# A decoder step on one core: key chunk and memory in quarters, logits between projections, a reordered top-k

## The reference

```python
m = rmsnorm(mem, g_mem)                    # 256 memory tokens
k = m @ w_k; v = m @ w_v
x = x + mixer(rmsnorm(x, g_mix), ...)      # spatial gate and short conv
x = x + cross_attn(rmsnorm(x, g_xattn), k, v, w_q, w_xo)
h = rmsnorm(x, g_moe)
logits = h @ w_router + b_router           # 32 experts
top_logit, top_e = lax.top_k(logits, 4); gates = softmax(top_logit)
# for each expert e: tokens gathered, then
gate, up = split(xb @ w1[e] + b1[e])
y = ((clip(up, -7, 7) + 1) * min(gate, 7) * sigmoid(1.702 * min(gate, 7))) @ w2[e] + b2[e]
x = x + sum over the 4 experts of gates * y
y = rmsnorm(x, g_final)
```

## Time and profile before

| what | value |
|---|---|
| median of 3 runs | 1243.08 us (1242.49 to 1243.96) |
| profiled execution | 1242.54 us, its span 1240.6 us |
| TensorE busy (PE) | 1162.7 us, 94% |
| VectorE busy (DVE) | 283.3 us, 23% |
| ACT busy | 166.0 us, 13% |
| moved by DMA | 458.5 MB, 370 GB/s on the mean |
| mean granted TensorE clock | 0.993 |
| chain that ended last | PE 50%, DMA 44%, DVE 4%, issue 2% |

### The profile page before, as it was taken

One profiled execution on the slowest core, in us unless ns is written; L12 is line 12 of the kernel. 1 busy time (PEld: TensorE's weight loads), 2 busy tenths in 40 slices (PEclk: granted clock), 3 DMA queues, 4 the chain that ended last, 5 costly groups with the idle time before them and its releaser, 6 DMA issues.

```text
span 1240.6 us, 14166 instructions
## 1 busy us (share of the span) xinstructions
PE 1162.7 (94%) x5620; PEld 618.5 (50%) x5620; DVE 283.3 (23%) x603; ACT 166.0 (13%) x267; POOL 29.6 (2%) x53
## 2 busy tenths in 40 slices
PE   8999999999999999999999999999999899989995
PEld 7888887775444444344444433333444343334433
DVE  5214532342111111111122111111111111111115
ACT  2011011021111111111111112111111111111112
POOL 1000000010000000000000000000000000000000
PEclk9999999999999999999999999999999999999998
DMA  9953334945999999999999999999999999999991
GB/s 372 409 176 136 130 143 169 427 189 213 417 428 427 426 428 428 427 427 427 427 428 427 428 427 427 428 427 429 427 428 427 426 429 427 428 428 426 429 402 57
DMA packets 37833, 458.53 MB, mean 370 GB/s; under 512 B 5744, under 2 KB 5744, under 8 KB 7056
## 3 DMA queue, kind: packets, MB, share of 16 engines
q1 hardware_dynamic: 35424, 454.11, 87.3%
q10 hardware_dynamic: 2352, 3.54, 0.8%
HBM read 454.41 MB, written 3.23 MB: 369 GB/s over the span
## 4 chain that ended last, share of the span: by engine, by line
PE 50%; DMA 44%; DVE 4%; issue 2%; SPq 0%; ACT 0%; DVEq 0%; ACTq 0%
DMA ring<-in_w_gu 43%; PE ps L1148 19%; PE ps L925 15%; PE ps L1195 6%; PE ps L943 2%; PE ps L1103 1%; PE ps L1123 1%; DVE arena L851 1%; PE ps L1178 1%; DMA ring<-in_w_k 1%; PE ps L1011 1%; PE ps L1042 1%; PE ps L1051 1%; PE ps L1021 1%; DVE arena L860 1%
## 5 line engine op out<-in xcount | busy, mean ns | idle before, releaser
L1148 PE MATMUL ps<-ring,arena 128*64 128x512 f32 x2048 | 456.3, 598 | 40.5 <-DMA ring<-in_w_gu 31.5
L1148 PEld LDWEIGHTS ps<-ring,arena 128*64 128x64 f32 x2048 | 144.7, 138 | 346.9 <-issue 279.9
L1195 PE MATMUL ps<-ring,arena 128*64 128x512 f32 x1024 | 226.8, 595 | 12.4 <-DVE arena L863 12.4
L830 DVE TENSOR_TENSOR resid<-resid,ps 128x264 f32<-128x264 f32 x128 | 51.2, 426 | 724.3 <-PE ps L1123 724.3
L925 PE MATMUL ps<-arena,ring 128*128 128x264 f32 (+1 forms) x832 | 186.6, 386 | 3.2 <-DMA ring<-in_w_k 1.8
L925 PEld LDWEIGHTS ps<-arena,ring 128*128 128x128 f32 x832 | 157.4, 190 | 30.8 <-DMA ring<-in_w_k 2.4
L1195 PEld LDWEIGHTS ps<-ring,arena 128*64 128x64 f32 x1024 | 70.7, 137 | 153.1 <-issue 127.9
L1103 PE MATMUL ps<-arena 128*128 128x256 f32 x432 | 99.0, 380 | 0.9 <-DVE arena L612 0.9
L545 ACT ACTIVATE arena<-ps 128x1024 f32<-128x1024 f32 x32 | 32.8, 1024 | 448.9 <-PE ps L1148 448.9
L1103 PEld LDWEIGHTS ps<-arena 128*128 128x128 f32 x432 | 82.6, 197 | 8.3 <-DVE arena L612 1.2
L1123 PE MATMUL ps<-arena 128*128 128x264 f32 x256 | 72.5, 396 | 0.0
(11 more groups left out here) (190 smaller groups left out, 419.5 us busy)
## 6 DMA issues: line engine op xcount, KB each, us to landing
ring<-in_w_gu SPq DMA_DIRECT2D x128, 2048.0 KB, 23.8
ring<-in_w_dn SPq DMA_DIRECT2D x64, 2048.0 KB, 20.4
ring<-in_w_in SPq DMA_DIRECT2D x10, 1024.0 KB, 28.3
ring<-in_kc SPq DMA_DIRECT2D x8, 1024.0 KB, 4.8
ring<-in_vc SPq DMA_DIRECT2D x8, 1024.0 KB, 4.9
ring<-in_w_v SPq DMA_DIRECT2D x4, 1024.0 KB, 24.7
ring<-in_w_out SPq DMA_DIRECT2D x4, 1024.0 KB, 5.4
ring<-in_w_q SPq DMA_DIRECT2D x4, 1024.0 KB, 4.8
```

Of the source, the lines that this page charges most:

```text
L830: TTN(resid[:, m, :], resid[:, m, :], ps[:, 6 + m % 2, 0:T], ALU.add).then_inc(c_added, 1)
L1148: last = mm(ps[64 * h:64 * h + 64, n, :], xg[:, cur, k, SLOTS * i:SLOTS * i + SLOTS], w[:, at:at + 512], start=(k == 0), stop=(k == KT - 1))
L1195: last = mm(ps[64 * h:64 * h + 64, 4, :], hid[:, k, :], w[:, at:at + 512], start=(k == 0), stop=(k == KT - 1))
```

## The change

The first key chunk comes in four quarters of two feature tiles, issued by SP; the memory comes in four quarters too, issued by ACT. TensorE makes key tiles 0 and 1 together, a quarter at a time. Seven warming matmuls stand in place of twelve. The router product of tile m - 1 stands behind attention output tile m. VectorE adds the square of tile m right behind its scaling. In the top-k, the scan starts from the count of larger logits, two steps are one, and the mask for rows that hold no token is replaced by a threshold of 1e30 in `top8`; slot numbers start at one, and the subtraction of one from the rank is gone. VectorE makes the one-hot matrix by token tiles, then the iteration count, and the gates after that; ACT's exponential stands behind its copies. TensorE loads the iteration count behind the first gather, and waits for the last copy of the gather only ahead of the third unit of the first expert (u == 3 of 0 to 3).

```diff
-            for half in range(2):
-                sp.dma_start(mem_raw[:, 4 * half:4 * half + 4, :], mem_t[:, 4 * half:4 * half + 4, :]).then_inc(mem_in[half], 16)
-                sp.dma_start(ring[:, 0, 1024 * half:1024 * half + 1024],
-                             w_k[0, :, 1024 * half:1024 * half + 1024]).then_inc(landed[0] if half else half_landed, 16)
+            for part in range(4):
+                sp.dma_start(ring[:, 0, 512 * part:512 * part + 512],
+                             w_k[0, :, 512 * part:512 * part + 512]).then_inc(landed[0] if part == 3 else part_landed[part], 16)
...
-            step(nc.gpsimd.iota(slot_i[:], pattern=[[1, SLOTS]], base=0, channel_multiplier=0))
+            step(nc.gpsimd.iota(slot_i[:], pattern=[[1, SLOTS]], base=1, channel_multiplier=0))
...
+            step(nc.gpsimd.memset(top8[:, 2, :], 1e30), top_filled)
...
+            for part in range(4):
+                act.dma_start(mem_raw[:, 2 * part:2 * part + 2, :], mem_t[:, 2 * part:2 * part + 2, :]).then_inc(mem_in[part], 16)
...
             for half in range(2):
-                act.wait_ge(mem_in[half], 16)
+                act.wait_ge(mem_in[2 * half], 16)
+                act.wait_ge(mem_in[2 * half + 1], 16)
...
-                if n == 3:
-                    act.wait_ge(ex_in, 1)
-                    nc.scalar.activation(ex[:], ex[:], ACT.Exp).then_inc(ex_out, 1)
                 act.wait_ge(grp, G[("htok", n)] + 1)
                 nc.scalar.activation(h_tok[0:rows, n // 2, 512 * (n % 2):512 * (n % 2) + 512], bank(("htok", n))[0:rows],
                                      ACT.Copy, scale=rstd_tok[0:rows, n // 2:n // 2 + 1]).then_inc(tok_copied, 1)
+            act.wait_ge(ex_in, 1)
+            nc.scalar.activation(ex[:], ex[:], ACT.Exp).then_inc(ex_out, 1)
             act.wait_ge(late_zero, 5)
...
-                dve.wait_ge(mem_in[k // 4], 16)
+                dve.wait_ge(mem_in[k // 2], 16)
...
-                if m:
-                    add_squares(sq, m - 1, 12)
-            add_squares(sq, KT - 1, 12)
+                add_squares(sq, m, 12)
...
+            dve.wait_ge(top_filled, 1)
             for t in range(TT):
-                ins = nc.vector.max(top8[:, t, :], lg[:, t, :])
+                rows = P if t < 2 else NS
+                ins = nc.vector.max(top8[0:rows, t, :], lg[0:rows, t, :])
                 ins.then_inc(dve_step, 1)
             steps[0] += TT
             dve.wait_ge(dve_step, steps[0])
-            TTN(ex[:], lg[:], top8[:, :, 0:1].to_broadcast([P, TT, NE]), ALU.subtract).then_inc(ex_in, 1)
             fourth = top8[:, :, TOPK - 1:TOPK].to_broadcast([P, TT, NE])
-            link(TTN(gt[:], lg[:], fourth, ALU.is_gt))
-            link(TTN(eq[:], lg[:], fourth, ALU.is_equal))
+            TTN(gt[:], lg[:], fourth, ALU.is_gt).then_inc(dve_step, 1)
+            TTN(eq[:], lg[:], fourth, ALU.is_equal).then_inc(dve_step, 1)
+            steps[0] += 2
+            dve.wait_ge(dve_step, steps[0])
             link(nc.vector.tensor_reduce(cnt3, gt[:], AX.X, ALU.add))
-            link(TS(cnt3, cnt3, -1.0, float(TOPK), ALU.mult, ALU.add))
             for t in range(TT):
-                ins = (nc.vector.tensor_tensor_scan(cum[:, t, :], ones[:, 0:NE], eq[:, t, :], 0.0, ALU.mult, ALU.add))
+                ins = nc.vector.tensor_tensor_scan(cum[:, t, :], ones[:, 0:NE], eq[:, t, :], cnt3[:, t:t + 1],
+                                                   ALU.mult, ALU.add)
                 ins.then_inc(dve_step, 1)
             steps[0] += TT
             dve.wait_ge(dve_step, steps[0])
-            link(TTN(cum[:], cum[:], bc(cnt3, 2, [P, TT, NE]), ALU.is_le))
-            link(TTN(eq[:], eq[:], cum[:], ALU.mult))
-            link(TTN(gt[:], gt[:], eq[:], ALU.add))
-            TTN(gt[:], gt[:], bc(valid[:], 2, [P, TT, NE]), ALU.mult).then_inc(sel_ready, 1)
+            link(STT(eq[:], cum[:], float(TOPK), eq[:], ALU.is_le, ALU.mult))
+            TTN(gt[:], gt[:], eq[:], ALU.add).then_inc(sel_ready, 1)
+            TTN(ex[:], lg[:], top8[:, :, 0:1].to_broadcast([P, TT, NE]), ALU.subtract).then_inc(ex_in, 1)
             dve.wait_ge(sel_ready, 1)
+            b = filled("rank", 128)
+            link(STT(rank[:], b[:, 0:96].rearrange("p (a e) -> p a e", a=TT), 1.0, gt[:], ALU.add, ALU.mult))
+            for t in range(TT):
+                TTN(hot(p_hot)[:, t], slot_no[:].unsqueeze(1).to_broadcast([P, 4, SLOTS]),
+                    rank[:, t, 0:4].unsqueeze(2).to_broadcast([P, 4, SLOTS]), ALU.is_equal).then_inc(first_p if t < 2 else p_built, 1)
+            nc.vector.tensor_reduce(cmax, b[:, 96:128], AX.X, ALU.max).then_inc(emptied, 7)
+            dve.wait_ge(emptied, G["rank"] + 1)
+            link(TTN(over, limits[:], cmax.to_broadcast([P, 4]), ALU.is_lt))
+            link(nc.vector.tensor_reduce(nover, over, AX.X, ALU.add))
+            TS(iters[:], nover[0:1, :], 4.0, 4.0, ALU.mult, ALU.add).then_inc(iters_ready, 1)
             dve.wait_ge(ex_out, 1)
...
-            link(STT(rank[:], b[:, 0:96].rearrange("p (a e) -> p a e", a=TT), 1.0, gt[:], ALU.add, ALU.mult))
-            TS(rank[:], rank[:], -1.0, None, ALU.add).then_inc(rank_ready, 1)
-            dve.wait_ge(rank_ready, 1)
-            build_p(0)
-            nc.vector.tensor_reduce(cmax, b[:, 96:128], AX.X, ALU.max).then_inc(emptied, 7)
-            dve.wait_ge(emptied, G["rank"] + 1)
-
-            link(TTN(over, limits[:], cmax.to_broadcast([P, 4]), ALU.is_lt))
-            link(nc.vector.tensor_reduce(nover, over, AX.X, ALU.add))
-            TS(iters[:], nover[0:1, :], 4.0, 4.0, ALU.mult, ALU.add).then_inc(iters_ready, 1)
...
-            for _ in range(12):
+            for _ in range(7):
                 mm(ps[:, 7, 0:P], ones[:], ones[:], start=True, stop=True)
-            for m in range(KT):
-                project("w_k", m, lambda k: mem[:, k, :], "k", (mem_ready, 0) if m == 0 else None)
-                if m == 1:
-                    pe.wait_ge(const_ready, CONSTS)
-                    sum_squares("mem_ssq", 1, NMEM, 2)
+            first_keys = ring[:, 0, :].rearrange("p (k n) -> p k n", k=KT)
+            for part in range(4):
+                pe.wait_ge(landed[0] if part == 3 else part_landed[part], 16)
+                pe.wait_ge(mem_ready, 2 * part + 2)
+                for m in range(2):
+                    for k in (2 * part, 2 * part + 1):
+                        last = mm(bank(("k", m))[:, 0:NMEM], first_keys[:, k, P * m:P * m + P], mem[:, k, :],
+                                  start=(k == 0), stop=(k == KT - 1))
+                    if part == 3:
+                        last.then_inc(grp, 1)
+            pe.wait_ge(const_ready, CONSTS)
+            sum_squares("mem_ssq", 1, NMEM, 2)
+            for m in range(2, KT):
+                project("w_k", m, lambda k: mem[:, k, :], "k")
...
+            def logits(k):
+                pe.wait_ge(h_ready, 2 * KT + k + 1)
+                return mm(bank("lg")[0:NE, 0:T], router[:, k, :], h_fm[:, k, :], start=(k == 0), stop=(k == KT - 1))
+
             for m in range(KT):
                 project("w_xo", m, lambda k: o_fm[:, k, :], "xo")
-            b = begin("lg")
-            for k in range(KT):
-                pe.wait_ge(h_ready, 2 * KT + k + 1)
-                last = mm(b[0:NE, 0:T], router[:, k, :], h_fm[:, k, :], start=(k == 0), stop=(k == KT - 1))
-            last.then_inc(grp, 1)
+                if m == 1:
+                    begin("lg")
+                if m:
+                    logits(m - 1)
+            logits(KT - 1).then_inc(grp, 1)
...
-            def gather(b, n):
+            def gather(b, n, first=False):
 
                 for half in range(2):
                     for t in range(TT):
+                        if first:
+                            pe.wait_ge(p_built if t == 2 else first_p, 1 if t == 2 else t + 1)
                         last = mm(b[:, 256 * half:256 * half + 256], h_tok[:, t, 256 * n + half:256 * n + 255 + half:2], p_hot[:, t, :],
                                   start=(t == 0), stop=(t == TT - 1))
                 return last
 
-            pe.wait_ge(p_built, 1)
             pe.wait_ge(late_zero, 5)
             pe.wait_ge(tok_copied, 6)
+            pe.wait_ge(first_p, 1)
             for n in range(4):
-                gather(begin(("ga", n)), n).then_inc(grp, 1)
+                gather(begin(("ga", n)), n, n == 0).then_inc(grp, 1)
+                if n == 0:
+                    pe.wait_ge(iters_ready, 1)
+                    end = pe.value_load(iters[0:1, 0:1], min_val=4, max_val=20)
             pe.wait_ge(bdn_in, 16)
-            pe.wait_ge(emptied, NG)
+            pe.wait_ge(emptied, NG - 1)
...
-            pe.wait_ge(iters_ready, 1)
-            end = pe.value_load(iters[0:1, 0:1], min_val=4, max_val=20)
...
+                        if j == 0 and u == 3:
+                            pe.wait_ge(emptied, NG)
```

21 lines of the change are left out of this document (6 added, 15 removed).

## The result

| kernel | median, lowest to highest | ratio of this to before, 95% interval |
|---|---|---|
| before, nine runs beside it | 1245.09 us, 1242.49 to 1247.94 | |
| changed, nine runs | 1253.30 us, 1249.07 to 1254.60 | 1.0063, 1.0051 to 1.0075 |

The changed kernel is slower. The profiled executions took 1253.3 and 1242.54 us, with spans of 1251.6 and 1240.6: 11.0 us between them, where the medians are 8.2 apart. The profiled execution of before is one of its quickest; what sets its spread of 5 us is not settled here.

A forecast was written before the change was run, and what follows sets the result against it. TensorE was taken to bound the front, DMA the expert loop. Head +0.3, tail -0.2 and clock +1.3 gave +1.4: 1243.9 us for the profiled execution, 1244.5 for the median, range 1241.8 to 1247.0.

The forecast's parts named there:

- The frame: Whole kernel: DMA bounds the expert loop, so the end is the loop's start plus a constant, moving one for one.
- memory's sum of squares: Head: its input is ready at 15.57 against TensorE's 15.33, so it starts 0.3 us later.
- half clock in the key tiles behind it: Head: not in the forecast; a rival had the clock fall after the 2.6 us wait, +1.5, 1246.0, chance 0.12.
- router products interleaved: Tail: same total for the products, but a new stall at the end makes the sum of squares 0.6 us later.
- shorter top-k, to the ranks: Tail, VectorE: instructions gone ahead of the selection save 1.1 us.
- gates and their transpose ahead of the gather: Tail: gates come after the one-hots, and their transpose holds up the gather; +2.4 us.
- half clock in the gather: Tail: TensorE's 3.5 us standstill halves the clock for 1.8 to 2.4 us of gather; +1.3 us.
- hole ahead of the loop: Between gather and expert loop: the 2.11 us hole goes, with count load and last copy hidden.
- the landing of the last memory quarter: Head: the last quarter lands at 10.2 to 11.4 us, taken as 10.6.
- memory rows starve: Head rival: ACT's queue gets the parameters' share, TensorE waits 3 to 5 us; 1246.5 to 1249.5, chance 0.10.
- The stall and the late squares: End of the attention output: last router product waits for VectorE, and the sum of squares comes 0.6 us later.
- the conditions named as proof against the forecast: Sum ready before 14, gather starting before 277, or a hole staying at the count's load.

The follow-up runs named there:

- h_act: Kernel before with only the new head (memory in quarters on ACT's queue, keys in quarters, seven warming matmuls), old tail: 1249.40 us, ratio 1.0042.
- t_lg: Changed kernel with the old head, router products back behind the last projection and the earlier adding of squares taken back: 1243.51 us, ratio 0.9987.
- t_two: Changed kernel with the old head, router products 0 to 5 together behind attention output tile 6, the others behind tile 7: 1245.23 us, ratio 1.0001.
- t_only: Changed kernel with the head of the kernel before (halves on SP, twelve warming matmuls, old key tile order): 1246.05 us, ratio 1.0008.
- best: Changed kernel, memory quarters on SP, memory's sum of squares behind key tile 3, router products behind last projection, gates' transpose behind gather: 1238.84 us, ratio 0.9949.

## Why the prediction was wrong

The frame held; a term at each end did not. The working of the prediction beside what the traces show, in us:

| step | forecast | measured |
|---|---|---|
| memory's sum of squares | +0.3 | +4.56 |
| half clock in the key tiles behind it | 0 (a rival: +1.5) | +1.8 |
| router products interleaved | +0.6 | +2.55 |
| shorter top-k, to the ranks | -1.1 | -0.95 |
| gates and their transpose ahead of the gather | +2.4 | +2.40 |
| half clock in the gather | +1.3 | +2.1 |
| hole ahead of the loop | -2.1 | -2.1 |
| loop start to the end (not explained) | 0 | +0.66 |
| sum | +1.4 | +11.0 |

**The step that failed** is the landing of the last memory quarter, "10.2 to 11.4; I take 10.6"; it came at 14.6. The term that was mis-sized is how much memory is left when the keys are done. The prediction put it at 0.14 MB, from the 0.6 us between the first issues of the two queues and equal shares from then on. The shares were equal (0.39 and 0.44 MB from 5 to 8), but the distance was 0.38 MB at 5.0, and 0.33 MB was left at 9.0, when SP's queue had moved 1.16 MB and so all but the last rows of the 1.05 MB of keys. The sharing beside the chunks was sized well at its slow bound: ACT's queue moved 0.17 MB in 2 us, 0.08 to 0.09 MB/us, against the parameters' 0.07. With 0.33 MB, that row gives 4.7 us and a landing near 13.7, an estimate; the prediction had it at 1.9 us for 0.14 MB, and took a value near the other bound. The rival "memory rows starve" named a landing of 12 to 16 and was given 0.10. Its landing was right, but by luck: it had ACT's queue starved "even beside the short key rows", and beside those the shares were equal. Why ACT's queue was so far behind at 5.0 isn't settled by a run.

**The second error** was to treat the rivals as if only one could come. A starved memory lengthens the wait for the sum, and a long wait is what lets the clock fall. With the late landing came the second fall, 4.56 + 1.8 together; the rival's price held the delay alone, up to 1249.5 (its own terms, a sum at 17 to 21, give 1245.9 to 1249.9), and the range ended at 1247.0. h_act shows that the fall isn't certain even then.

**The third** was a term put at nothing. "The same total" for products that are moved between others is true of their own durations, not of the changes between them: six detours at 0.3 us, 1.6 to 1.7 in all, which t_lg and t_two isolate. The trace of before has one change to 32 columns, at 264.42, where nothing made it stand out. The stall and the late squares, forecast at 0.6, measure about 0.7 (0.97 less one detour).

**The low clock in the gather** came as forecast in kind. The size was short: the forecast had 1.8 to 2.4 us of work at half speed (worth 0.9 to 1.2, where it took 1.3), and the granted clock was low for 6.8 us (284.4 to 291.2; the windows at its ends, 284 to 285 and 291 to 292, have 0.71 and 0.88), some of it standstill, but with 5 us of matmuls and transposes in it (0.50 from 286 to 291). In the other kernels with a low stretch the gather took 12.21 to 12.77 instead of 10.6, so 1.6 to 2.2 more.

**What was right**: the last Square and the reduce end last ahead of the memory's sum of squares, with TensorE idle 2.39; the last router product waits for VectorE (0.42); the gates' transpose, not the one-hot, releases the gather, 3.47 us after the ranks; the loading of the loop count and the wait for the last copy are hidden and their hole gone (which of the two made it, no run tells); VectorE's saving in the top-k is 0.95; and the ratio of one to one between loop start and end. The +2.40 for the gates is exact in part by luck: 0.3 of it is half clock in the gates' transposes, and in t_only, where they run at full clock, it is 2.12. None of the conditions named as proof against the forecast was met, which says that they watched for a gain and not for the loss.

The Trainium skill's rule on gaps ("TensorE: Matmul & The Clock Gate", Why this matters for your kernels), against holes above about 3 us, speaks of the 3.47 us hole, and the trace agrees (0.50 in the gather). It doesn't cover the fall after 2.39 us in the changed kernel, nor the one in best after 1.04; there the rows decide.

Of the medians' 8.2 us between the kernels, h_act alone has 4.8 and t_only 1.5. The rest, about 2, isn't assigned by medians. In the traces the parts add up to 3.15 + 6.0 = 9.1 of the loop start's 10.3: the changed kernel's head is 0.4 later than h_act's (a landing 1.3 earlier, and the fall), and its tail 0.9 longer than t_only's, with the clock low for longer.
